# The even mixer's input projection as three products of high and low halves, contraction block outermost

## The chip, the cores and the metric

The kernel runs on one core of a Trainium2 chip. The metric is the device time of one execution in microseconds (us), the median of three runs. Besides these runs there is one profiled execution, from which all rows below come. In the profile PE is the TensorE matmul, PEld its weight load, DVE is VectorE, ACT is ScalarE, POOL is GpSimd and SP is SyncE, which issues most of the transfers.

## The reference

The model has two layers over 384 tokens, 128 context tokens and 256 latent tokens, with 1024 channels. What matters here is the first step of the even layer:

```
h  = x * (1 + scale) + shift              # scale, shift from SiLU(cond) @ ada_w + ada_b
u  = h @ w_in                             # (384 x 1024) @ (1024 x 2048)
ux, ub, uc, up = split(u, 512 columns each)
ya = ub * conv3(uc * ux, conv_w)          # depthwise, width 3
yb = pool_mixer(up, pool_w, pool_scale)   # windowed means minus the token
out = concat(ya, yb) @ w_out
```

After it come a residual with LayerNorm, a dense SwiGLU, the odd layer (latent attention beside a Fourier mixer) and a top-2-of-8 mixture of experts. All inputs are float32.

## The kernel before, in words

Each engine has its own instruction stream, written out by hand, and semaphores tie the streams together. Nothing is planned at run time around the change; the order in each stream is the order of the code.

**Tiles.** `HT` holds the modulated tokens turned, as 8 contraction blocks (`KD` = 8) of 128 channels by 384 tokens. `w_in` comes as four units ("evin", 0 to 3) of 512 columns each, 2 MB a unit, in the order of `EV_ORDER`: first the pooled columns `up`, then `ux`, `ub` and `uc`. The ring `WR` has four slots. Units 0 and 2 lie in slot 3, units 1 and 3 in slot 1. Between them SP loads the 3 MB panels of `ada_w` ("ada", n) and then `w_out` ("evout", 0 and 1). A load into a slot waits until PE has signalled that the slot's last unit is used up (`free`, `release`).

**PE.** `evin(t, ks)` (L2142) multiplies output tile t (128 columns of `w_in` by 384 tokens, one PSUM bank) over the contraction blocks `ks`, in float32. The matmul shows as two records in the trace. The loop from L2167 takes the tiles t = 0 to 15 in turn, all blocks of one tile before the next tile. The first three tiles (`EV_EARLY`) start with blocks 0 to 3, since blocks 4 to 7 of the tokens depend on a later panel: between the first and the second of them stands `ada_turn(2)`. After each unit of four tiles PE does a panel of the modulation (`ada_turn`, L2080, and `ada_mm`, L2106), and after unit 2 also the four matmuls of the pooling mixer (L2190). Then follows `project_out` (L2209).

**ACT.** It modulates the latent tokens in two halves (L1041), then waits for each of the tiles 0 to 11 and copies it out of PSUM (L1048, L1052), then scales the pooled tiles (L1056).

**DVE.** It modulates the context tokens in two halves (L1484), turns the panels into modulation columns (`ada_stage`, L1351 and L1353; `ada_cols`, L1343), multiplies tiles 12 to 15 into the convolution's input (L1503) and does the convolution (L1511 to L1515).

**POOL.** It computes the pooling (L866 to L872) as soon as the tiles 0 to 3 are copied, zeroes rows in memory (L876, L878), stores the first gate (L831) and then loads the LayerNorm gain, bias and the gates (`ln_params(0, 0)`, L841 to L843). It waits for the gate's store alone before these three loads.

**The split products of the feed-forward network.** The SwiGLU that follows already works on halves: ACT casts a weight piece to the rounded type fp32r (the high half, L1065), DVE subtracts it from the float32 piece (the low half, L1538), the same is done with the tokens (L1095, L1554), and `product` (L2240) does three matmuls, high by high, high by low and low by high (L2244 to L2246). Its first two blocks of columns are computed with the contraction block outermost (`first_gate_up`), four PSUM banks in turn.

Of the kernel before, what the change touches and what calls it, by code (L numbers as in the profile page):

```python
# [279 lines left out]
def build(nc, x_prompt, x_sample, cache_ckv, cache_kpe, c, c_ctx, ada_w, ada_b, ln_g, ln_b, ev_w_in, ev_conv_w,  # L280
# [4 lines left out]
    with ctx:  # L285
# [68 lines left out]

        SIL, HF = carve(TOK, TOK)
# [229 lines left out]
        EV_EARLY = 3  # L585
# [36 lines left out]
        def _(sp):  # L622
# [15 lines left out]
            def raw_free(n, more=0):  # L638

                if isinstance(n, int) and n < RING:  # L640
                    return
                sp.wait_ge(lo_done, n - (RING - 1) + more)
# [91 lines left out]
            sp.wait_ge(lo_done, FF_LAST[0] + 1)  # L734
# [88 lines left out]
        def _(pool):  # L823
# [152 lines left out]
        def _(act):  # L976
# [58 lines left out]
            for half in range(2):  # L1035
# [8 lines left out]
            for t in range(12):  # L1044
                act.wait_ge(u_ps, t + 1)
                if t >= 4:
                    dst = (UX, UB)[t // 4 - 1]
                    nc.scalar.copy(dst[:, t % 4, :], PS[:, t % 4, 0:TOK]).then_inc(u_act, 1)  # L1048
                else:
                    act.wait_ge(z_pad, 2)  # L1050
                    for tok, at, n in SEGU:
                        last = nc.scalar.copy(UP[:, t % 4, at:at + n], PS[:, t % 4, tok:tok + n])  # L1052
                    last.then_inc(u_act, 1)
            for g in range(NPOOL):
                act.wait_ge(pm_ps, g + 1)
                nc.scalar.activation(MIX[:, 4 + g, :], PS[:, 4 + g % 2, 0:TOK], ACT.Identity,  # L1056
                                     scale=COLS[:, 12 + g:13 + g]).then_inc(mix_pool, 1)

            def high(piece, used_up):
# [3 lines left out]
                if used_up is not None:  # L1063
                    act.wait_ge(w_used, used_up)
# [255 lines left out]
        def _(dve):  # L1320
# [166 lines left out]

            ada(range(2))
# [45 lines left out]
            def low(piece):  # L1534

                n, at, _ = piece
                dve.wait_ge(hi_done, n + 1)
# [14 lines left out]
            for k in range(KD):  # L1552
                dve.wait_ge(hx_hi, k + 1)
# [500 lines left out]
        def _(pe):  # L2054
# [65 lines left out]
            def release(ins, name):  # L2120


                ins.then_inc(used[ring.units[name][0]], 1)
# [18 lines left out]
            def evin(t, ks):  # L2142

                w = slot(("evin", t // 4))[:, 0:4096].rearrange("p (k n) -> p k n", k=KD)
                for k in ks:
                    last = mm(PS[:, t % 4, 0:TOK], w[:, k, (t % 4) * P:(t % 4 + 1) * P], HT[:, k, :],  # L2146
                              start=(k == 0), stop=(k == KD - 1))
                    if t in (4, 8, 12) and k == 0:
                        release(last, ("ada", 2 + t // 4))
                return last  # L2150
# [7 lines left out]
            pe.wait_ge(ht_a, 1)  # L2158
            pe.wait_ge(ht_d, 1)
            wait_unit(pe, ("evin", 0))  # L2160
            evin(0, range(4))
            ada_turn(2, True)
            for t in range(1, EV_EARLY):
                evin(t, range(4))
            h_ready(0)

            for t in range(16):  # L2167
                if t % 4 == 0 and t:
                    wait_unit(pe, ("evin", t // 4))
                if t >= 4:  # L2170
                    pe.wait_ge(u_act, t - 3)
                evin(t, range(4 if t < EV_EARLY else 0, KD)).then_inc(u_ps, 1)
# [67 lines left out]
            def product(out, left, right, start, stop):  # L2240


                (lh, ll), (rh, rl) = left, right
# [537 lines left out]
```

## Time and profile before

| | us |
|---|---|
| median of three runs | 1333.41 |
| the three runs | 1337.09, 1333.41, 1333.41 |
| profiled execution, its time | 1337.3 |
| profiled execution, its span | 1335.4 |
| PE busy in the span | 1278.3 |
| DVE busy | 715.0 |
| ACT busy | 521.6 |
| POOL busy | 131.2 |

The span is the time from the first to the last instruction. Matmuls are pipelined: the busy time of one lies partly over that of the next, so the pace of a stream is read from the starts of its matmuls and not from their durations. The mean granted TensorE clock is 0.975 of full speed.

### The profile page before, as it was taken

How to read it: one execution, taken by the hardware profiler on the slowest of the kernel's cores; microseconds unless marked ns; L12 is line 12 of the kernel's file. 1: busy time of each engine (PE TensorE's matmuls, PEld its weight loads, DVE VectorE, ACT ScalarE, POOL GpSimd, SP SyncE). 2: the span in 40 equal slices, each digit the busy share in tenths (PEclk: the TensorE clock that was granted, in tenths of full speed). 3: DMA queues.
4: the chain of work that ended last, by engine and by line, in shares of the span. 5: the costliest groups of instructions: out<-in, count | busy, mean ns of one | idle time of the engine just before them, and what ended most of it. 6: DMA issues, size and time to landing. Idle time of an engine off the chain costs nothing.

```text
span 1335.4 us, 17338 instructions
## 1 busy us (share of the span) xinstructions
PE 1278.3 (96%) x6503; PEld 959.3 (72%) x6504; DVE 715.0 (54%) x1026; ACT 521.6 (39%) x632; POOL 131.2 (10%) x119
## 2 busy tenths in 40 slices
PE   4999999999999989999999999999999999999994
PEld 2555449999999964677646886765467878888882
DVE  1101456334234252555335777743256788888888
ACT  0101025233233242234202746533136666777772
POOL 0420003200000033000000010100102021202020
PEclk8999999999999989899998789999999999999997
DMA  9986386424324184720405666859989899999993
GB/s 365 351 340 247 107 319 190 158 95 161 122 94 157 47 320 144 263 78 24 173 0 194 243 228 257 294 193 341 352 317 338 293 338 357 383 366 385 362 358 142
DMA packets 125356, 317.10 MB, mean 237 GB/s; under 512 B 12931, under 2 KB 47078, under 8 KB 124774
## 3 DMA queue, kind: packets, MB, share of 16 engines
q1 hardware_dynamic: 119264, 295.00, 60.7%
q0 software_dynamic: 5744, 21.07, 5.1%
q8 instruction: 43, 0.70, 0.2%
q14 instruction: 27, 0.22, 0.1%
q10 hardware_dynamic: 278, 0.10, 0.0%
HBM read 306.37 MB, written 9.76 MB: 237 GB/s over the span
## 4 chain that ended last, share of the span: by engine, by line
PE 89%; DVE 5%; DMA 3%; issue 1%; SPq 1%; ACT 1%; DVEq 0%; ACTq 0%
PE ps L2546 10%; PE ps L2547 10%; PE ps L2548 10%; PE ps L2244 8%; PE ps L2246 8%; PE ps L2245 8%; PE ps L2209 7%; PE ps L2552 7%; PE ps L2146 6%; PE ps L2336 3%; DMA sb_ring<-in_ev_w_in 2%; PE ps L2106 2%; PE ps L2438 1%; PE ps L2080 1%; DVE sb_expert_lo L1753 1%
## 5 line engine op out<-in xcount | busy, mean ns | idle before, releaser
L1753 DVE TENSOR_TENSOR sb_expert_lo<-sb_expert_raw,sb_expert_hi 128x1792 fp32r<-128x1792 f32 (+1 forms) x210 | 334.1, 1646 | 85.0 <-PE ps L2552 73.7
L1201 ACT CAST sb_expert_hi<-sb_expert_raw 128x1792 fp32r<-128x1792 f32 (+1 forms) x210 | 283.4, 1392 | 117.3 <-PE ps L2548 78.4
L2546 PE MATMUL ps<-sb_expert_hi,sb_expert_x 128*128 128x448 f32 x448 | 166.9, 373 | 4.5 <-DVE sb_expert_lo L1753 2.5
L2547 PE MATMUL ps<-sb_expert_lo,sb_expert_x 128*128 128x448 f32 x448 | 165.3, 369 | 0.0
L2548 PE MATMUL ps<-sb_expert_hi,sb_expert_x 128*128 128x448 f32 x448 | 165.0, 368 | 0.0
L2244 PE MATMUL ps<-sb_split_acts,sb_split_weights 128*128 128x384 f32 x352 | 118.0, 335 | 0.4 <-issue 0.4
L2246 PE MATMUL ps<-sb_split_acts,sb_split_weights 128*128 128x384 f32 x352 | 117.9, 335 | 0.0
L2245 PE MATMUL ps<-sb_split_acts,sb_split_weights 128*128 128x384 f32 x352 | 117.7, 334 | 0.0
L2546 PEld LDWEIGHTS ps<-sb_expert_hi,sb_expert_x 128*128 128x128 f32 x448 | 85.2, 190 | 20.1 <-issue 12.7
L2548 PEld LDWEIGHTS ps<-sb_expert_hi,sb_expert_x 128*128 128x128 f32 x448 | 85.0, 190 | 7.2
L2547 PEld LDWEIGHTS ps<-sb_expert_lo,sb_expert_x 128*128 128x128 f32 x448 | 85.1, 190 | 7.0
L1547 DVE TENSOR_TENSOR sb_scratch<-sb_scratch,ps 128x384 f32<-128x384 f32 x22 | 12.2, 554 | 142.7 <-PE ps L2246 120.4
L1538 DVE TENSOR_TENSOR sb_split_weights<-sb_ring,sb_split_weights 128x1024 fp32r<-128x1024 f32 x66 | 80.7, 1282 | 7.1 <-ACT sb_split_weights L1065 7.1
L2146 PE MATMUL ps<-sb_ht,sb_ring 128*128 128x384 f32 x256 | 83.7, 487 | 0.6 <-DMA sb_ring<-in_ev_w_in 0.6
L2546 PE MATMUL ps<-sb_expert_hi,sb_expert_h 128*128 128x512 f32 x196 | 78.7, 401 | 0.7 <-DVE sb_expert_lo L1753 0.7
L2547 PE MATMUL ps<-sb_expert_lo,sb_expert_h 128*128 128x512 f32 x196 | 77.1, 393 | 0.0
L2548 PE MATMUL ps<-sb_expert_hi,sb_expert_h 128*128 128x512 f32 x196 | 77.1, 393 | 0.0
L2146 PEld LDWEIGHTS ps<-sb_ht,sb_ring 128*128 128x128 f32 x256 | 48.3, 190 | 35.7 <-issue 2.8
L1065 ACT CAST sb_split_weights<-sb_ring 128x1024 fp32r<-128x1024 f32 x66 | 65.1, 1056 | 5.7 <-PE ps L2246 5.7
L2244 PEld LDWEIGHTS ps<-sb_split_acts,sb_split_weights 128*128 128x128 f32 x352 | 66.1, 188 | 1.3 <-issue 0.5
L2245 PEld LDWEIGHTS ps<-sb_split_acts,sb_split_weights 128*128 128x128 f32 x352 | 66.1, 188 | 0.9
L2246 PEld LDWEIGHTS ps<-sb_split_acts,sb_split_weights 128*128 128x128 f32 x352 | 66.1, 188 | 0.0
(339 smaller groups left out, 1835.5 us busy)
## 6 DMA issues: line engine op xcount, KB each, us to landing
sb_expert_raw<-in_moe_w_gate SPq DMA_DIRECT2D x128, 448.0 KB, 5.6
sb_expert_raw<-in_moe_w_up SPq DMA_DIRECT2D x128, 448.0 KB, 7.0
sb_expert_raw<-in_moe_w_down SPq DMA_DIRECT2D x112, 512.0 KB, 7.3
sb_ring<-in_ada_w SPq DMA_DIRECT2D x14, 3072.0 KB, 17.7
sb_ring<-in_ffn_w_gate SPq DMA_DIRECT2D x44, 256.0 KB, 3.8
sb_ring<-in_ffn_w_up SPq DMA_DIRECT2D x44, 256.0 KB, 4.7
sb_ring<-in_ffn_w_down SPq DMA_DIRECT2D x22, 512.0 KB, 6.3
sb_ring<-in_ev_w_in SPq DMA_DIRECT2D x4, 2048.0 KB, 15.4
```

Source lines behind the costliest of these rows:

```text
L1201: nc.scalar.copy(EHI[piece.h][:, 0:w], ERAW[:, r, 0:w]).then_inc(e_hi, 1)
L1538: V.tensor_tensor(WS[:, at, 1, :], RAW[:, at, :], WS[:, at, 0, :].bitcast(F32), ALU.subtract)\
L1753: V.tensor_tensor(ELO[r][:, 0:w], ERAW[:, r, 0:w], EHI[piece.h][:, 0:w].bitcast(F32), ALU.subtract)\
L2146: last = mm(PS[:, t % 4, 0:TOK], w[:, k, (t % 4) * P:(t % 4 + 1) * P], HT[:, k, :], start=(k == 0), stop=(k == KD - 1))
L2209: last = mm(PS[:, 2 * g + h, :], lhs(k)[:, g * P:(g + 1) * P], w[:, k % per, h * 512:(h + 1) * 512], start=(k == 0), stop=(k == n - 1))
L2244: first = mm(out, lh, rh, start=start, stop=False)
L2245: mm(out, lh, rl, start=False, stop=False)
L2246: return first, mm(out, ll, rh, start=False, stop=stop)
L2546: first = mm(out, lh, rh, start=start, stop=False)
L2547: mm(out, lh, rl, start=False, stop=False)
L2548: return first, mm(out, ll, rh, start=False, stop=stop)
L2552: made = [mm(out, left, right, start=start, stop=stop) for out, right in zip(outs, rights)]
```

## The change

The projection of the even mixer is computed with `product` too. ACT casts each of the 8 blocks of tokens to a high half, in the place of the gate rows and the LayerNorm gain (`EVX[0]`), and DVE writes the low half in place over `HT` (`EVX[1]`). Of each weight block (128 by 512) the high half goes to one of four spare places in the unit's own ring slot, and the low half in place over the raw block. The loops of PE are turned: the contraction block is outermost and the four tiles of a unit, in four PSUM banks, innermost. The first pass over blocks 0 to 3 still takes only three tiles, and the fourth follows once the second half of the tokens is ready. ACT may cast block k of 4 to 7 of a unit only once PE has used up block k - 4 (`w_used`). The counters `hi_done`, `lo_done`, `w_used` and `hx_lo`, which the feed-forward network uses, start later by constants. On POOL the loads of `ln_params(0, 0)` wait until all 16 tiles are done.

```diff
+        EVX = tuple(nc.alloc_sbuf_tensor_at(f"sb_input_{part}", [P, KD, TOK], F32R, offset=at)
+                    for part, at in (("hi", gb_at), ("lo", ht_at)))
+        EVW = {at: tuple(nc.alloc_sbuf_tensor_at(f"sb_input_w_{part}{at}", [P, n, 512], F32R, offset=ring_at + 4 * (SLOT * at + col))
+                         for part, n, col in (("hi", 4, 4096), ("lo", KD, 0))) for at in (1, 3)}
+        EV_SPLITS, EV_FREED = 4 * KD, 16
...
@@ ln_params (POOL)
+                else:
+                    pool.wait_ge(u_ps, 16)
...
@@ ACT
+            def input_high(half):
+                act.wait_ge(ht_a, half + 1)
+                act.wait_ge(ht_d, half + 1)
+                for k in range(4 * half, 4 * half + 4):
+                    nc.scalar.copy(EVX[0][:, k, :], HT[:, k, :]).then_inc(hx_hi, 1)
+            def input_w_high(u, ks):
+                for k in ks:
+                    if k == 0:
+                        wait_unit(act, ("evin", u))
+                    if k >= 4:
+                        act.wait_ge(w_used, 4 * u + k - 3)
+                    hi, _, raw = input_w(u, k)
+                    nc.scalar.copy(hi, raw).then_inc(hi_done, 1)
...
+            modulate_sample(0)
+            input_high(0)
+            input_w_high(0, range(4))
+            modulate_sample(1)
+            input_high(1)
+            input_w_high(0, range(4, KD))
+            for u in range(1, 4):
+                input_w_high(u, range(4))
+                input_out(u - 1)
+                if u == 3:
...
+                input_w_high(u, range(4, KD))
...
@@ DVE
+            def input_w_low(u, ks):
+                for k in ks:
+                    dve.wait_ge(hi_done, KD * u + k + 1)
+                    hi, lo, raw = input_w(u, k)
+                    V.tensor_tensor(lo, raw, hi.bitcast(F32), ALU.subtract).then_inc(lo_done, 1)
             ada(range(2))
             modulate_prompt(0)
-            ada(range(2, 3))
+            input_low(0)
+            ada_stage(2)
+            input_w_low(0, range(2))
+            ada_cols(2)
+            input_w_low(0, range(2, 3))
             modulate_prompt(1)
+            input_w_low(0, range(3, 4))
+            input_low(1)
+            input_w_low(0, range(4, KD))
+            input_w_low(1, range(4))
             ada_stage(3)
+            input_w_low(1, range(4, KD))
             ada_cols(3)
+            input_w_low(2, range(4))
             ada_stage(4)
+            input_w_low(2, range(4, KD))
             ada_gate(0, 5)
             ada_cols(4)
+            input_w_low(3, range(4))
             ada_stage(5)
+            input_w_low(3, range(4, KD))
...
@@ PE
-            def evin(t, ks):
-                w = slot(("evin", t // 4))[:, 0:4096].rearrange("p (k n) -> p k n", k=KD)
-                for k in ks:
-                    last = mm(PS[:, t % 4, 0:TOK], w[:, k, (t % 4) * P:(t % 4 + 1) * P], HT[:, k, :],
-                              start=(k == 0), stop=(k == KD - 1))
+            def evin(u, k, tiles=range(4)):
+                pe.wait_ge(lo_done, KD * u + k + 1)
+                if u == 0:
+                    pe.wait_ge(hx_lo, k + 1)
+                hi, lo, _ = input_w(u, k)
+                for t in tiles:
+                    if u and k == 0:
+                        pe.wait_ge(u_act, 4 * u + t - 3)
+                    cols = slice(t * P, (t + 1) * P)
+                    first, last = product(PS[:, t, 0:TOK], (hi[:, cols], lo[:, cols]), (EVX[0][:, k, :], EVX[1][:, k, :]),
+                                          k == 0, k == KD - 1)
...
+                    if k == KD - 1:
+                        last.then_inc(u_ps, 1)
+                if k < 4 and t == 3:
+                    last.then_inc(w_used, 1)
             ada_mm(2)
-            evin(0, range(4))
+            evin(0, 0, range(3))
             ada_turn(2, True)
-            for t in range(1, EV_EARLY):
-                evin(t, range(4))
+            for k in range(1, 4):
+                evin(0, k, range(3))
             h_ready(0)
-            for t in range(16):
...
+            for k in range(4):
+                evin(0, k, (3,))
+            for t in range(3, 16, 4):
+                for k in range(4 if t == 3 else 0, KD):
+                    evin(t // 4, k)
```

## Rows read from the trace of the kernel before

**Rows 1.** The page, busy time of the engines: us, share of the span, instructions.

```profile
PE 1278.3 (96%) x6503; PEld 959.3 (72%) x6504; DVE 715.0 (54%) x1026; ACT 521.6 (39%) x632; POOL 131.2 (10%) x119
```

**Rows 2.** Chain of waits up to 240 us: start, duration, what held the chain.

```profile
12.93 26.58 DMA sb_ring<-in_ev_w_in
39.65 2.82 PE ps L2146 x8
...
61.86 2.72 PE ps L2106 x32
64.58 20.84 PE ps L2146 x64
...
117.51 20.65 PE ps L2146 x64
138.19 0.63 DVE sb_scratch L1503 x2
...
147.44 13.93 PE ps L2209 x32
```

**Rows 3.** Stretches of the four units, L2146 alone: stretch, busy by engine, PEclk, DMA.

```profile
39.65:61.86 22.21, 21.12 (x64) 11.97 (x64) 1.00 1.01 375
sum 84.54, PE 83.43 PEld 47.79; mean PE 20.86 PEld 11.95
```

**Rows 4.** PE in order of time in the feed-forward network: start, duration, matmul.

```profile
215.06 0.33 PE L2244 MATMUL ps<-sb_split_acts,sb_split_weights 128*128 128x384 f32 x1
...
220.26 0.39 PE L2244 MATMUL ps<-sb_split_weights,sb_split_hidden 128*128 128x512 f32 x1
```

**Rows 5.** Groups by line and shape, weight loads, 203 to 260 us.

```profile
L2245 PEld LDWEIGHTS ps<-sb_split_acts,sb_split_weights 128*128 128x128 f32 x80 | 15.0, 188 | 0.1
```

**Rows 6.** Four stretches, PE alone: stretch, busy, PEclk (granted clock), DMA share, GB/s.

```profile
203.50:210.00 6.50, 6.46 (x37) 1.00 0.69 196
485.00:492.00 7.00, 5.14 (x24) 0.55 1.03 362
...
200.00:204.00 4.00, 2.40 (x23) 1.00 0.65 191
```

**Rows 7.** One line each, ACT and DVE: duration ns min/median/max, first and last start.

```profile
L1065 ACT CAST sb_split_weights<-sb_ring x26: 1037/1049/1159, 202.1 to 299.5; 128x1024 fp32r<-128x1024 f32 x26
L1095 ACT CAST sb_split_acts<-sb_ht x8: 615/622/628, 201.3 to 207.0; 128x384 fp32r<-128x384 f32 x8
L1538 DVE TENSOR_TENSOR sb_split_weights<-sb_ring,sb_split_weights x24: 1215/1219/3416, 203.3 to 298.9; 128x1024 fp32r<-128x1024 f32 x24
L1554 DVE TENSOR_TENSOR sb_split_acts<-sb_ht,sb_split_acts x8: 550/552/559, 201.9 to 209.1; 128x384 fp32r<-128x384 f32 x8
```

**Rows 8.** DVE in order of time, 39 to 45 us.

```profile
43.73 0.17 DVE L1343 TENSOR_TENSOR sb_mod_cols<-ps,sb_mod_bias 128x12 f32<-128x12 f32 x1 [4.07 <-PE ps L2080]
43.94 1.37 DVE L1484 TENSOR_SCALAR sb_ht<-ps,sb_mod_cols 128x128 f32<-128x128 f32 x4
```

**Rows 9.** POOL in order of time: first and last pooling step, an LN load.

```profile
52.30 0.87 POOL L866 TENSOR_TENSOR sb_scratch<-sb_scratch 128x415 f32<-128x415 f32 x1 [15.19 <-ACT sb_scratch L1052]
...
70.73 1.26 POOL L872 TENSOR_TENSOR sb_scratch<-sb_scratch 128x128 f32<-128x128 f32 x2
...
114.28 0.53 POOL L843 DMA_DIRECT2D sb_gate_rows<-gate_rows  x1
```

**Rows 10.** Transfers by issue: KB each, us to landing (the last LN load).

```profile
sb_gate_rows<-gate_rows POOLq DMA_DIRECT2D x1, 1024.0 KB, 14.3
```

**Rows 11.** The issue of unit 1 at 33.5 us: issue, and its time to landing.

```profile
L630 SPq DMA_DIRECT2D sb_ring<-in_ev_w_in x1: 2601/2601/2601, 33.5 to 33.5; - x1
DMA to landing us min/median/max: 22.6/22.6/22.6
```

**Rows 12.** DVE, L1538 while POOL works, 222 to 230 us: duration ns min/median/max.

```profile
L1538 DVE TENSOR_TENSOR sb_split_weights<-sb_ring,sb_split_weights x2: 3187/3302/3416, 222.7 to 225.8; 128x1024 fp32r<-128x1024 f32 x2
```

**Rows 13.** The issue of evout 1 at 140 us: issue, and its time to landing.

```profile
L630 SPq DMA_DIRECT2D sb_ring<-in_ev_w_out x1: 368/368/368, 140.2 to 140.2; - x1
DMA to landing us min/median/max: 7.8/7.8/7.8
```

More of the change, by code:

```diff
@@ L1033, in squares, with modulate_sample @@
                     .then_inc(sd_ready, 1)
-            for half in range(2):
+            def modulate_sample(half):
                 act.wait_ge(xt_t, 2 * NG)
@@ L1043, in _ @@
                 last.then_inc(ht_a, 1)
[L1044 to L1053, printed above, removed]
@@ new lines, in input_w_high, with input_out @@
+            def input_w_high(u, ks):
[6 more added lines that the diff above has]
+                    nc.scalar.copy(hi, raw).then_inc(hi_done, 1)
+            def input_out(u):
+                for t in range(4 * u, 4 * u + 4):
+                    act.wait_ge(u_ps, t + 1)
+                    if u:
+                        dst = (UX, UB)[u - 1]
+                        nc.scalar.copy(dst[:, t % 4, :], PS[:, t % 4, 0:TOK]).then_inc(u_act, 1)
+                    else:
+                        act.wait_ge(z_pad, 2)
+                        for tok, at, n in SEGU:
+                            last = nc.scalar.copy(UP[:, t % 4, at:at + n], PS[:, t % 4, tok:tok + n])
+                        last.then_inc(u_act, 1)
@@ new lines, in _ @@
+            modulate_sample(0)
[8 more added lines that the diff above has]
+                if u == 3:
+                    for g in range(NPOOL):
+                        act.wait_ge(pm_ps, g + 1)
+                        nc.scalar.activation(MIX[:, 4 + g, :], PS[:, 4 + g % 2, 0:TOK], ACT.Identity,
+                                             scale=COLS[:, 12 + g:13 + g]).then_inc(mix_pool, 1)
+                input_w_high(u, range(4, KD))
@@ L2141, in _, with product @@
             pe.wait_ge(sc_ready, 1)
-            def evin(t, ks):
-                w = slot(("evin", t // 4))[:, 0:4096].rearrange("p (k n) -> p k n", k=KD)
-                for k in ks:
-                    last = mm(PS[:, t % 4, 0:TOK], w[:, k, (t % 4) * P:(t % 4 + 1) * P], HT[:, k, :],
-                              start=(k == 0), stop=(k == KD - 1))
-                    if t in (4, 8, 12) and k == 0:
-                        release(last, ("ada", 2 + t // 4))
-                return last
+            def product(out, left, right, start, stop):
+                (lh, ll), (rh, rl) = left, right
+                first = mm(out, lh, rh, start=start, stop=False)
+                mm(out, lh, rl, start=False, stop=False)
+                return first, mm(out, ll, rh, start=False, stop=stop)
+            def evin(u, k, tiles=range(4)):
[9 more added lines that the diff above has]
+                                          k == 0, k == KD - 1)
+                    if u and (t, k) == (0, 0):
+                        release(first, ("ada", 2 + u))
+                    if k == KD - 1:
+                        last.then_inc(u_ps, 1)
+                if k < 4 and t == 3:
+                    last.then_inc(w_used, 1)
             ada_mm(0)
@@ L2237, in _ @@
             h_ready(1)
-            def product(out, left, right, start, stop):
-                (lh, ll), (rh, rl) = left, right
-                first = mm(out, lh, rh, start=start, stop=False)
-                mm(out, lh, rl, start=False, stop=False)
-                return first, mm(out, ll, rh, start=False, stop=stop)
             def halves(buf, *at):
```

42 lines of the change are left out of this document (19 added, 23 removed).

## Prediction

> **What bounds the kernel now.** I read the busy times first: PE is at work in 96% of the span, DVE in 54%, ACT in 39%, POOL in 10% [rows 1]. So only what shortens PE's own stream, or a wait of PE, moves the time. Next the chain of waits up to 240 us: from 39.65 us, when the first unit of `w_in` has landed, to 138.16 us it is PE alone, four units of projection (the last takes 20.65 us) with panels between (2.72 us for 32 records of `ada_mm`) [rows 2]. Then comes a short stretch on DVE, which prepares the convolution, and PE goes on with `project_out` at 147.44 us. Third the stretches of the four units: their matmuls keep PE busy for 83.43 us, at full granted clock in the one shown [rows 3]. That is the term the change works on. There are 16 tiles x 8 blocks = 128 float32 matmuls in it, so one costs 83.43 / 128 = 0.652 us.
>
> **What three products cost.** The same shape (128x128 weights, 384 columns, fp32r) runs in the feed-forward network. From the matmul that starts at 215.06 us to the one at 220.26 us there are 30 of them, ten products of three [rows 4]: 5.20 / 30 = 0.173 us a matmul, 0.520 us a product. The printed 0.33 us is the latency of one, of which half lies under its neighbour; three times that would be 1.0 us and would forecast a loss, and it is not the pace. 128 products take 66.6 us. PE saves 83.4 - 66.6 = 16.9 us.
>
> The bounds of this term: if the weight load sets the pace, at 188 ns a load [rows 5], the 384 matmuls take 72.2 us and the saving is 11.2. Those loads too start every 0.173 us in the feed-forward stream, or the pace of rows 4 could not hold, so I take 0.173.
>
> The new loop goes through four PSUM banks in each block. The stretch 203.5 to 210 us has that very order (`first_gate_up`), and its granted clock is 1.00, the 2.4 GHz level [rows 6]. The Trainium skill speaks against the order: its page "TensorE: Matmul & The Clock Gate", section "A second HAM failure mode: psum-queue depth-cycling", says that going through banks in each iteration can leave small idle times that make the clock swing between its levels. By the row the products cost 66.6 us; by the rule a part of them would run at half clock (a rival below). By the rule, this trace doesn't agree: the row shows no swing.
>
> **The splits.** There are 32 casts and 32 subtractions of 128x512, and 8 of each of 128x384. Casts take 0.622 us at 384 and 1.049 at 1024 columns, subtractions 0.552 and 1.219 [rows 7]; in between, 0.71 and 0.69 us for 512. ACT gets some 28 us of work and DVE some 26 us, over the 84 us of the stretch, in which DVE and ACT are mostly idle. PE takes 4 x 0.520 = 2.08 us for a block, each splitter 0.7, so in the steady state the halves are ready early: block k + 4 may be cast when block k is used up, which leaves it 3 x 2.08 = 6.2 us for 0.33 + 0.71 + 0.69 = 1.7 us of work. They cost nothing there. If that cover were gone, each of the 16 blocks with k of 4 to 7 would put up to 1.7 us on PE.
>
> *At the start* nothing covers them. The unit lands at 39.6 us; PE now waits for the first cast and subtraction, 0.71 + 0.69 = 1.4 us. Nearest rows from both sides: 1.17 (two ops of 384 columns) and 2.27 (two of 1024) [rows 7]. I take 1.4. The tokens' halves 0 to 3 are done before the weights land.
>
> *The rest of unit 0.* PE: block 0 on three tiles to 42.6, `ada_turn(2)` to 43.8, blocks 1 to 3 on three tiles by 48.5. DVE's `ada_cols(2)` was at 43.73 and comes near there again, then one subtraction, then the context half, 1.37 us [rows 8], then block 3's subtraction, ready at some 46.9; PE wants it at 46.9. The fourth tile's blocks 0 to 3 run 48.5 to 50.6, and block 4's cast waits for the first of them: 48.5 + 0.52 + 0.33 + 0.71 + 0.69 = 50.75. I put 0.25 us on this unit; the bounds are 0 and 1.0 (one split more in front). It then ends at 59.1 instead of 61.8.
>
> *Unit ends.* All four tiles now finish within the last 2.1 us of a unit, and the next unit's first block wants the banks copied out. ACT's copies are below 0.622 us each [rows 7], four are below 2.5 us, the first starts 1.2 us before the end, and PE has 2.72 us of `ada_mm` at least between units [rows 2]. Nothing is added while ACT is not held up. But ACT now stands at unit u + 1's first cast ahead of the copies of unit u. Unit 1 landed at 33.5 + 22.6 = 56.1 us [rows 11], four casts end by 59, and the first copy is due at 57.9: late by 1.1, inside the panel. Units 2 and 3 have 10 us more slack, since their issue moves forward with PE.
>
> *DVE's order.* `ada_cols(3)` and `ada_cols(4)`, which wait for PE's panels, now have the next unit's first subtractions queued behind them. `ada_cols(3)` comes 2.72 us before unit 2 starts, enough for three of 0.69 us. Cost 0. What waits behind the new waits for `hi_done` is `ada_stage`, used only after the next unit.
>
> *POOL beside DVE.* The pooling lay at 52.3 to 72.0 us [rows 9]; with all four tiles copied only after unit 0 it starts some 6 us later and runs beside unit 1's subtractions. While POOL worked, L1538 took 3.19 to 3.42 us instead of 1.22 [rows 7, 12]. A subtraction of 512 would then take up to 1.7 to 2 us. DVE does one per 2.08 us of PE there, with four blocks of lead: cost 0. The Trainium skill, "GPSIMD Engine Reference", section "Key points", says that GpSimd shares its SBUF interfaces with VectorE and contends with instructions that have two SBUF inputs, as these subtractions have. Its rule and the row agree on the stretching; it weighs in a rival below.
>
> *After unit 3.* The four products into the convolution's input (0.63 us a tile [rows 2]) were spread over the unit; now they come at its end, 0.52 us apart. The last ends about 1.1 us after PE instead of 0.65. I put 0.45 us, with bounds 0 and 1.9 (three of them wholly late).
>
> *POOL's new wait.* The LayerNorm loads move behind unit 3's end, the last from 114.3 to some 124 us. The last took 14.3 us and landed at 128.6 [rows 9, 10]; now at 138. What reads it is the residual after the first third of `project_out`, which ends at 147.44 + 13.93 = 161.4 before, 146.6 then. 8 us remain. What queues behind it is only the second gate's store. These loads now run beside evout 1, issued 2 us after unit 3 and landed 7.8 us later [rows 13]: 125.1 + 7.8 = 132.9 alone. With all 14.3 us in front of it, 139.4; its rows are wanted halfway through the first 13.93 us of `project_out`, at 139.6. Cost 0, bound 2.
>
> **Sum.** -16.9 + 1.4 + 0.25 + 0.45 = -14.8 us. After 138 us every wait, load and store is timed from PE's progress, so the gain goes through. The profiled execution took 1337.3 us (span 1335.4), which gives 1322.5. It stands 3.9 above the median of the runs; that is the highest of the three too, 1337.09. From the median, 1333.4 - 14.8 = 1318.6.
>
> **Rivals.**
> *One clock dip at the start.* PE's pause before unit 0 grows by 1.4 us. The stretch 485 to 492 us, in which PE was busy for 5.14 of 7 us, ran at a granted clock of 0.55 [rows 6]: 7 x 0.45 = 3.2 us lost, 1321.8. Against it stands 200 to 204 us, busy for 2.40 of 4 us and at 1.00.
> *The weight load sets the pace:* 5.6 us more, 1324.2.
> *Late halves.* ACT and DVE are in-order queues; with the spare high places freed by PE, the cast after that and the subtraction last (stretched beside POOL), PE could end in step with them on the 16 late blocks. At 0.7 us a block 11.2 us are lost, 1329.8, no change. At the full 1.73 it is 27.7, which gives +12.9 and 1346.3: slower. It decides from 14.8 / 16 = 0.93 us a block. For it speaks only the row of 3.4 us; against it the lead of 6.2 us, and that POOL's work ends in unit 2.
> *The clock swings* between 1.2 and 2.4 GHz through the products: at half the time slow, 33 us more, 1352. This is what the row 203.5 to 210 speaks against. By the rule of the Trainium skill's page "TensorE: Matmul & The Clock Gate" cited above, this is the outcome.
>
> **How the numbers follow.** Forecast 0.76, dip 0.09, weight load 0.03, late halves shallow 0.03 (still faster) and 0.04 (no change), in step 0.03, swinging clock 0.02. A measurement can tell 0.3%, 4 us, from no change. Faster: 0.76 + 0.09 + 0.03 + 0.03 = 0.91; same 0.04; slower 0.05. The range: the low end is the whole 16.9 us and 2 us of luck with clock dips elsewhere, 1314.5; the high end takes in the dip and the weight-load pace with 1 us, 1325.5.
>
> **What would show it.** Starts of L2245 0.173 us apart in the units; each of units 1 to 3 lasting 16.6 us; PE's pause before unit 0 longer by 1.4 us; the first `ada_mm` after unit 0 at 59 and unit 3's end at 123 us; no wait of PE for the halves longer than 0.3 us; granted clock 1.00. It would be wrong if idle time before PE's products sums to more than 3 us, if the pace is 0.19, or if a later stage (evout 1, the gate rows) begins to wait.

## The result, and the profile after

| | before | after |
|---|---|---|
| median, six runs each, us | 1335.25 | 1326.41 |
| lowest and highest, us | 1331.6, 1339.34 | 1324.09, 1328.77 |
| profiled execution: time, span, mean clock | 1337.3, 1335.4, 0.975 | 1324.09, 1322.3, 0.971 |
| project_out starts in the profile, us | 147.4 | 134.4 |

The ratio of the runs is 0.9928, with a 95% interval of 0.9906 to 0.9951: 8.8 us faster, where 14.8 were forecast. 1326.4 lies just above the range, which ended at 1325.5. With all the runs of this study the changed kernel has a median of 1326.9 (18 runs) and the kernel before one of 1337.4 (125 runs, 1330.2 to 1341.9), so the gain is 10.5 us. The 1333.4 from which the forecast started was the median of three favourable runs; 4.0 us of the miss in absolute time come from there, and 4.3 from the gain.

The chain of waits of the changed kernel up to 135 us (start, duration, what held the chain) answers to [rows 2].

```profile
38.32 0.52 ACT sb_input_hi L1066
38.86 1.28 DVE sb_input_lo L1540 x3
40.27 0.55 DVE sb_input_lo L1540
40.83 0.47 DVE sb_mod_stage L1399
41.29 0.47 DVE sb_mod_stage L1401
41.76 0.61 DVE sb_input_w_lo L1547
42.41 0.45 PE ps L2219
...
60.86 2.72 PE ps L2180 x32
...
123.87 2.01 DVE sb_scratch L1577 x7
...
134.49 13.93 PE ps L2294 x32
```

Ahead of unit 0 the chain isn't the landing any more. It goes through the token halves, then the two panel copies, then the first low half of the weights, all on DVE and one behind the other. The first product starts at 42.41 us, 2.76 us after the 39.65 of the kernel before.

The units themselves, PE alone (stretch, busy, PEclk, DMA share, GB/s), answer to [rows 3].

```profile
42.41:60.79 18.38, 18.38 (x109) 1.00 1.04 385
63.50:80.27 16.77, 16.77 (x100) 1.00 0.81 310
84.31:101.07 16.76, 16.76 (x101) 1.00 1.03 388
108.08:125.02 16.94, 16.94 (x99) 1.00 0.62 246
```

Units 1 to 3 take 16.8 to 16.9 us instead of 20.7 to 20.8. Unit 0 holds a part of a panel besides its products (18.4 us, 22.2 before). The pace is the forecast one, as the starts of PE in order of time show (start, duration, matmul):

```profile
50.14 0.33 PE L2219 MATMUL ps<-sb_input_hi,sb_input_w_hi 128*128 128x384 f32 x1
50.31 0.33 PE L2220 MATMUL ps<-sb_input_lo,sb_input_w_hi 128*128 128x384 f32 x1
50.48 0.33 PE L2221 MATMUL ps<-sb_input_hi,sb_input_w_lo 128*128 128x384 f32 x1
50.66 0.33 PE L2219 MATMUL ps<-sb_input_hi,sb_input_w_hi 128*128 128x384 f32 x1
```

0.52 us for a product, 0.173 us a matmul. The groups by line and shape from 38 to 140 us (busy, mean ns, idle before) show the splits and the only idle time of PE before a product:

```profile
L2219 PE MATMUL ps<-sb_input_hi,sb_input_w_hi 128*128 128x384 f32 x128 | 43.6, 341 | 1.3 <-DVE sb_input_w_lo L1547 1.3
...
L1547 DVE TENSOR_TENSOR sb_input_w_lo<-sb_ring,sb_input_w_hi 128x512 fp32r<-128x512 f32 x32 | 21.8, 714 | 24.9 <-ACT sb_input_w_hi L1076 24.9
L1076 ACT CAST sb_input_w_hi<-sb_ring 128x512 fp32r<-128x512 f32 x32 | 18.3, 619 | 32.3 <-PE ps L2221 26.2 <-DMA sb_ring<-in_ev_w_in 6.1
```

In this profile the start of project_out has moved by 12.95 us and the span by 13.1. So the single pair of profiles shows 13 of the forecast 14.8 us, and the medians 10.5. The pair flatters the change: the changed kernel's profiled execution, 1324.1, is the fastest of its first six, and that of the kernel before, 1337.3, is a usual one. The granted clock differs too: the changed kernel's 18 runs have a mean clock of 0.970, and those of the kernel before (119 whose clock is on record) 0.973.

### The profile page after: what moved, and what is told of

Read it like the earlier page. It is cut to its first block, busy times and chain, and to the rows that moved or that the text cites. A ratio compares the mean times of both kernels' runs of the same rounds, so it can differ in the third digit from the quotient of the medians.

```text
span 1322.3 us, 17688 instructions
## 1 busy us (share of the span) xinstructions
PE 1265.0 (96%) x6631; PEld 979.9 (74%) x6632; DVE 739.4 (56%) x1066; ACT 543.4 (41%) x672; POOL 132.6 (10%) x119
## 4 chain that ended last, share of the span: by engine, by line
PE 89%; DVE 5%; DMA 3%; issue 1%; ACT 1%; SPq 0%; DVEq 0%; ACTq 0%
PE ps L2623 10%; PE ps L2219 10%; PE ps L2624 10%; PE ps L2625 10%; PE ps L2221 10%; PE ps L2220 10%; PE ps L2294 7%; PE ps L2629 7%; PE ps L2413 3%; PE ps L2180 2%; PE ps L2154 2%; DMA sb_ring<-in_ada_w 1%; PE ps L2515 1%; DVE sb_expert_lo L1827 1%; PE ps L2511 1%
## 5 line engine op out<-in xcount | busy, mean ns | idle before, releaser
L2221 PEld LDWEIGHTS ps<-sb_split_acts,sb_split_weights 128*128 128x128 f32 x352 | 66.6, 189 | 0.0
L928 POOL TENSOR_TENSOR sb_scratch<-sb_constants 1x1 f32<-1x1 f32 x19 | 18.1, 953 | 466.3 <-DVE sb_static_rows L1850 297.7
```

Of the source, the lines that this page charges most:

```text
L2221: return first, mm(out, ll, rh, start=False, stop=stop)
```

## The experiments

"Tail" is the time from project_out's first matmul to the end of the span. "Half clock" is the time in the tail at the 1.2 GHz level, summed from the trace's record of the granted clock. Both are of the profiled execution. The median is of all runs of that kernel, and so is the last column: the half-clock time in the whole span, worked out for each run from its span and mean clock, 2 x (1 - clock) x span, and averaged. "Runs beside it" are those of the kernel before that were made together with a version and to which its ratio refers; their medians lie between 1336.9 and 1338.4 us.

| kernel (labels) | median (runs) | unit 0 starts | panel after unit 0 | project_out | tail | half clock | half clock, whole span, all runs |
|---|---|---|---|---|---|---|---|
| before | 1337.4 (125) | 39.65 | 61.79 | 147.37 | 1188.1 | 57.8 | 71.3 |
| before again (e2) | | 40.93 | 63.11 | 148.69 | 1189.4 | 65.4 | |
| before, third (e15) | | 39.76 | 61.98 | 147.56 | 1190.6 | 66.0 | |
| before, fourth (e16) | | 41.25 | 63.42 | 149.00 | 1189.4 | 65.1 | |
| after | 1326.9 (18) | 42.41 | 60.79 | 134.42 | 1187.8 | 59.6 | 79.6 |
| after again (e1) | | 40.95 | 62.49 | 136.13 | 1189.8 | 65.3 | |
| after, third (e11) | | 42.51 | 60.91 | 134.55 | 1189.4 | 61.3 | |
| order only (e3) | 1336.9 (12) | 41.32 | 63.49 | 149.07 | 1189.6 | 65.4 | 71.4 |
| pause only (e10) | 1335.5 (12) | 42.59 | 64.74 | 150.32 | 1183.8 | 47.4 | 63.6 |
| before + filler (e6) | 1333.6 (12) | 39.02 | 61.17 | 146.75 | 1184.8 | 52.8 | 57.1 |
| after + filler (e5) | 1321.8 (6) | 40.28 | 60.21 | 133.85 | 1185.6 | 53.5 | 65.1 |
| after, DVE order (e8) | 1323.2 (12) | 41.64 | 60.04 | 133.68 | 1188.2 | 62.2 | 71.8 |
| the same again (e12) | | 41.61 | 60.01 | 133.66 | 1186.0 | 56.1 | |
| block 0 float32 (e4) | 1319.4 (10) | 39.02 | 57.88 | 131.52 | 1184.0 | 49.9 | 65.1 |
| the same again (e7) | | 41.37 | 60.23 | 133.86 | 1184.1 | 47.9 | |
| block 0 float32 + filler (e9) | 1321.3 (6) | 38.98 | 57.81 | 131.45 | 1181.9 | 45.8 | 63.8 |
| after + 1.3 us of work (e13) | 1326.0 (6) | 41.17 | 59.58 | 134.61 | 1183.7 | 46.6 | 71.5 |
| after + 2.6 us of work (e14) | 1325.2 (6) | 40.88 | 62.47 | 138.79 | 1181.4 | 42.4 | 69.7 |
| block 0 float32 + 1.3 us (e17) | 1323.9 (6) | 39.32 | 58.18 | 133.22 | 1188.9 | 61.3 | 74.5 |

The tail goes with its half-clock time. A straight line through the 19 profiles is 1166.2 + 0.36 x half clock, and no profile lies more than 1.0 us off it. The seven profiles of the kernel before and its versions and the twelve of the changed kernel and its versions lie on the same line (mean distance 0.0 for both). So no later stage got slower for good with the change: at the same half-clock time the tail is as long as before.

**e1 and e11, the changed kernel again.** No edit.

> The changed kernel once more, for a second profile and more times. The first profiles differ by 13.1 us in span, the medians by 8.8. Theory C (clock): the work of PE is shortened by 13 us, and 3 to 5 us of it are given back in single executions by stretches at half clock (mean granted clock 0.969 to 0.971 in the changed kernel's runs, 0.975 in the profile of the kernel before). Then PE reaches project_out at 134.5 +- 1 us again, the times lie at 1324 to 1329, and a longer run has a lower mean clock: about 1.3 us for each 0.001. Rival N (noise of few runs): the gain of the medians moves to 12 or 13 us with more runs. Rival O (another stage got slower for good): the second profile shows a stage outside the projection that is longer by several us at full clock.

> The changed kernel a third time, for a third profile. Theory: either PE starts unit 0 late (42.4 us, panels at half clock, order on DVE) or in time (41 us) and runs its first blocks at half clock; both ways the panel after unit 0 starts at 60.8 to 62.5 us where my sum had 59.1, and project_out at 134.4 to 136.2. Median 1327 +- 1. If the start is not the cause, this profile shows a panel at 59.1 +- 0.5 us and still a time of 1325 or more.

e1: median 1327.6, ratio 0.9925 (0.9909 to 0.9941). e11: 1326.3, ratio 0.9926 (0.9904 to 0.9948). The first result was no accident, the noise rival falls. What I had not expected is what e1 shows at the start. PE alone, two stretches (stretch, busy, PEclk, DMA share, GB/s), first in e1:

```profile
24.00:41.00 17.00, 13.52 (x89) 0.70 1.04 392
41.00:49.00 8.00, 8.00 (x32) 0.57 1.02 374
```

and in the first profile of the changed kernel:

```profile
24.00:41.00 17.00, 15.80 (x88) 0.51 1.04 392
41.00:49.00 8.00, 6.66 (x46) 1.00 1.03 376
```

There are two ways to lose. Either the panels before unit 0 run at half clock, the tokens are modulated later, and PE starts at 42.4 us. Or PE starts at 40.95, 1.4 us after the landing as in my sum, and its first blocks run mostly at half clock: the clock is 0.57 from 41 to 49 us, ahead of which PE had paused for 1.95 us. The panel after unit 0 starts at 60.8, 60.9 and 62.5 us where the sum had 59.1. e13 and e14 have the same start, and their profiles add to this: e14 repeats e1 (pause of 1.95 us, clock 0.57, panel at 62.5), while e13 loses in neither way. There PE paused longest, 3.65 us, and the clock stayed up in unit 0, as this stretch of PE alone shows:

```profile
41.00:49.00 8.00, 7.83 (x49) 1.00 1.03 376
```

Its unit 0 starts at 41.17 and its panel at 59.6, nearly as forecast. So the length of the pause doesn't say whether the clock falls after it; what does is open.

**e2, e15, e16, the kernel before again.** No edit.

> The kernel before once more, for a second profile. Theory C: the places and number of half-clock stretches differ from the first profile (31 to 39 us, 486, 544, 725, 752, 776, 1315, 1325 us), the span by up to 4 us, all of it inside such stretches; project_out starts at 147.4 +- 1. Rival N: the span comes out near 1333 to 1336 and the clock does not explain the differences. The ratio of its times to the kernel before is 1.000 +- 0.002.

> The kernel before a third time, for a third profile: where its project_out starts (147.4 and 148.7 so far) and how long its tail is (1188.1 and 1189.4). If the tail of the kernel before is the same as the changed kernel's on the average, project_out must start at 146.5 or so for the medians to differ by 10.5 only; by theory T its mean tail is 2 to 3 us shorter, so here 1184 to 1187 with less than 57 us of half-clock time.

> The kernel before a fourth time, same question and same numbers.

Its four profiles have project_out at 147.4 to 149.0, 148.2 on the average; the changed kernel's three have 134.4 to 136.1, 135.0. So 13.1 us are gained there. The two tails of 1190.6 and 1189.4 miss what I had expected of e15 and e16. But the three profiled executions of e2, e15 and e16 lie at the slow end of their own runs (1340 us against a median of 1337.4), so they say little about the usual tail. From the medians, less the 1.8 us that an execution's time lies above its span, the usual tail is 1337.4 - 1.8 - 148.2 = 1187.4 us before and 1326.9 - 1.8 - 135.0 = 1190.1 after. That is worked out, not seen.

**e3, the order of the loops alone**, in float32.

```diff
-            for t in range(16):
-                if t % 4 == 0 and t:
+            for k in range(4):
+                evin(0, k, (3,))
+            for t in range(3, 16, 4):
+                if t > 3:
                     wait_unit(pe, ("evin", t // 4))
...
-                evin(t, range(4 if t < EV_EARLY else 0, KD)).then_inc(u_ps, 1)
+                for k in range(4 if t == 3 else 0, KD):
+                    evin(t // 4, k)
```

> One part of the change alone: the loops of the projection are turned (contraction block outermost, four banks), with float32 matmuls on the unsplit tokens and weights, no splits and no later LayerNorm loads. If the order by itself costs something (rival: bank switching, tiles that finish together), units 0 to 3 take longer than 20.9 us each and the kernel is slower than before by 1 us or more. By my sum the order costs only the convolution's input at the end: +0.2 to +0.5 us, units at 20.9 us, time within 1 us of the kernel before.

Median 1336.9, ratio 0.9993 (0.9977 to 1.0009). PE alone in units 1 to 3:

```profile
66.21:86.95 20.74, 20.74 (x68) 1.00 0.83 320
91.00:111.74 20.74, 20.74 (x68) 1.00 0.65 247
119.05:139.69 20.64, 20.64 (x66) 1.00 0.75 299
```

As expected: going through four banks costs nothing and the clock stays at 1.00. The Trainium skill, "TensorE: Matmul & The Clock Gate", section "A second HAM failure mode: psum-queue depth-cycling", describes a bfloat16 kernel whose clock swings when it goes through the banks in each iteration. This case's traces don't show that, neither in float32 (1.00 here) nor in the products (1.00 in the four units above).

**e5 and e6, a filler in PE's idle time** ahead of the second panel, in the changed kernel and in the one before.

```diff
             x_turned(0)
+            for _ in range(7):
+                mm(PS[:, 6, 0:384], ident, X[:, 0, 0:384], start=True, stop=True)
             ada_mm(1, None, 0)
```

> The changed kernel with seven more float32 matmuls (128x128 by 128x384, some 0.65 us each, into a PSUM range that the next panel overwrites) in PE's idle time between the turned tokens and the landing of the second panel (19.5 to 24.4 us). Theory C (clock): the half-clock stretches between 24 and 41 us, and the one at 42 to 49 us that one profile of the changed kernel shows, come from this idle time and from the pause before unit 0. With the filler the clock stays at 1.00 up to about 39 us, the panels before unit 0 end at 38 us, PE starts the first product 1.0 to 2.0 us earlier than in the changed kernel's profiles (40.95 and 42.41 us), project_out starts at 132.5 to 134, and the median falls by 1.5 to 3 us. Rival (the landing of unit 0 and the order on DVE alone hold the start): project_out starts at 134.4 or later and the median moves by less than 1 us.

> The same filler in the kernel before. There PE waits for the landing of unit 0 at 39.6 us whatever its clock was, unless it is late (40.93 us in one profile). Theory C: the first matmul of unit 0 starts at 39.6 us, project_out at 147.4 us; the median falls by 0 to 1.3 us, less than in the changed kernel, since the float32 matmuls hang on the landing alone. Rival (the clock lottery is the same for both kernels and has nothing to do with the start): both kernels move by the same amount.

e5: 1321.8, ratio 0.9899 (0.9875 to 0.9922). e6: 1333.6, ratio 0.9981 (0.9964 to 0.9998). In e5, PE alone:

```profile
24.00:33.00 9.00, 5.99 (x57) 1.00 1.03 398
33.00:41.00 8.00, 5.20 (x35) 0.76 1.04 384
41.00:49.00 8.00, 8.00 (x44) 0.82 1.03 376
```

The filler holds the clock at 1.00 to 33 us, and later it still falls twice. The three profiles with the filler (e5, e6, e9) have 3.4 to 6.8 us at half clock ahead of unit 0, the sixteen without it 10.2 to 20.5. The start gets better by 1.2 to 1.4 us in both kernels, against the averages of their profiles. But the medians fall by 5.1 and 3.8 us, more than the start explains. In the kernel before I had expected at most 1.3; against the runs beside it the fall is 2.5 us, and its interval, 0.3 to 4.8, does not exclude that. The rest is in the tails, 1185.6 and 1184.8.

**e8 and e12, another order on DVE before unit 0.**

```diff
-            input_low(0)
-            ada_stage(2)
-            input_w_low(0, range(2))
+            input_low(range(1))
+            input_w_low(0, range(1))
+            ada_stage(2)
+            input_low(range(1, 4))
+            input_w_low(0, range(1, 2))
```

> The changed kernel with another order on DVE before unit 0: low half of token block 0, low half of weight block 0, then the panel copies (ada_stage of panel 2), then the low halves of token blocks 1 to 3. Theory S (the order on DVE holds the start): PE's first product starts at 41.0 us at either clock level, up to 1.4 us earlier than in the profile with 42.4; project_out starts 0.5 to 1.4 us earlier and the median is 0.5 to 1.5 us lower than the changed kernel's 1327.3. Rival: PE reaches unit 0 only at 41.0 us when its clock is halved, so the order on DVE gives at most 0.3 us, and the wait moves behind block 0, to the panel copies.

> The other order on DVE once more: its six times spread from 1316 to 1327 us. Theory S: the median stays 2 to 5 us under the changed kernel's, PE starts unit 0 within 0.3 us of the end of its panel or 1.4 us behind the landing, whichever is later. Rival: the first median of 1323.2 was luck, and it is back at 1326 or more.

1323.2, ratio 0.9895 (0.9865 to 0.9925), and 1322.9, ratio 0.9899 (0.9876 to 0.9923). DVE in order of time in e8:

```profile
39.13 0.56 DVE L1540 TENSOR_TENSOR sb_input_lo<-sb_ht,sb_input_hi 128x384 fp32r<-128x384 f32 x1 [1.20 <-ACT sb_input_hi L1066]
40.89 0.69 DVE L1547 TENSOR_TENSOR sb_input_w_lo<-sb_ring,sb_input_w_hi 128x512 fp32r<-128x512 f32 x1 [1.20 <-ACT sb_input_w_hi L1076]
41.50 0.55 DVE L1399 COPY sb_mod_stage<-ps 128x384 f32<-128x384 f32 x1
41.97 0.55 DVE L1401 COPY sb_mod_stage<-ps 128x384 f32<-128x384 f32 x1
```

The first low half of the weights comes 0.9 us earlier than the 41.8 of the changed kernel, the panel copies go under the products, and PE starts at 41.6. The panel after unit 0 starts at 60.0 instead of 60.8. So the order on DVE did hold the start. It gives 3.7 us in the median, 0.8 us of it ahead of project_out (133.7 against 134.5 at the same early clock).

**e4, e7 and e9, block 0 of unit 0 in float32**, with and without the filler.

```diff
+                if (u, k) == (0, 0):
+                    for t in tiles:
+                        last = mm(PS[:, t, 0:TOK], input_w(0, 0)[2][:, t * P:(t + 1) * P], HT[:, 0, :], start=True, stop=False)
+                    if t == 3:
+                        last.then_inc(w_used, 1)
+                    return
...
             input_w_low(0, range(4, KD))
+            dve.wait_ge(w_used, 1)
+            input_low(range(1))
```

> The changed kernel with block 0 of unit 0 multiplied in float32 from the unsplit tokens and weights, so that PE needs no halves to start; the token block is split after that for units 1 to 3. Theory S (start): in the changed kernel PE started its first product at 42.4 us, 2.8 us after the landing, held by the chain of token halves, panel copies and first weight halves on DVE. Then PE starts at 39.6 to 41.1 us here, pays 4 x 0.13 us more for the block, and project_out starts 1 to 2 us earlier than in the changed kernel, the time is 1 to 2 us lower. Rival: the start is not what is missing, later waits in unit 0 (the tokens' second half, block 4) take the time back, and project_out starts within 0.4 us of the changed kernel's 134.5.

> The kernel with block 0 of unit 0 in float32 once more, since its four times lay 8 us below the changed kernel where its start explains 3 to 4.5 us (project_out at 131.5 instead of 134.4 and 136.1). Theory C: the other 4 to 5 us were shorter half-clock stretches (mean clock 0.976 instead of 0.9695), which depend on the pauses of PE before unit 0 for 1 or 2 us and on luck for the rest, so the median rises to 1320 to 1323. Rival: the float32 start changes the later stretches for good, and the median stays at 1319 +- 1 with a clock of 0.976.

> Both remedies at once: block 0 of unit 0 in float32, and the seven filler matmuls at 19.5 us. Theory C: the clock is mostly at 1.00 before unit 0 and PE starts at the landing, 39.0 to 39.6 us, in each execution, so project_out starts at 131.5 +- 0.5 and the median is 0 to 2.5 us under the 1319.7 of float32 block 0 alone. Rival (each remedy repairs the same loss, the rest is luck of the clock): 1319.7 +- 1.

1319.0 and 1319.7, ratios 0.9872 (0.9851 to 0.9894) and 0.9877 (0.9851 to 0.9903), all ten runs 1319.4: the fastest version here, 18.0 us under the kernel before. PE no longer waits for a half before unit 0: it starts at the landing (e4, 39.0) or when its own panel ends (e7, 41.4). The start of project_out is 131.5 or 133.9, by the clock before 41 us. Again the median gains more (7.5 us on the changed kernel) than the start (0.6 to 4.6), and the tails are short, 1184. e9, with both remedies, has the shortest span of all in its profile (1313.3) and yet no better median, 1321.3 (1315.2 to 1324.8), ratio 0.9895 (0.9873 to 0.9917).

**e10, the pause alone.** The kernel before, with a copy and a subtraction between the landing and PE's first matmul; their results are not used.

```diff
+                if half == 0:
+                    wait_unit(act, ("evin", 0))
+                    nc.scalar.copy(SCR[:, 0:512], slot(("evin", 0))[:, 0:512]).then_inc(pause_a, 1)
...
+            dve.wait_ge(pause_a, 1)
+            V.tensor_tensor(SCR[:, 512:1024], slot(("evin", 0))[:, 0:512], SCR[:, 0:512], ALU.subtract).then_inc(pause_d, 1)
...
+            pe.wait_ge(pause_d, 1)
```

> The kernel before with the start's pause alone: after the landing of unit 0 ACT copies its first block and DVE subtracts it, both into scratch that nothing reads, and PE waits for the subtraction before its first float32 matmul. Nothing is computed from them. By my sum the pause costs its own 1.4 us: project_out at 148.8 to 149, time +1.4 us. Theory C (a longer pause before unit 0 brings half-clock time after it, as in the second profile of the changed kernel): project_out at 149 to 151, the median 2 to 5 us above the kernel before, the mean clock lower by 0.001 to 0.003. Rival (pause hidden since PE's panel ends at 41 us in most executions): +0 to +0.7 us.

Median 1335.5, ratio 0.9995 (0.9982 to 1.0008), that is -2.4 to +1.1 us against the runs beside it. This contradicts my sum (+1.4) and theory C (+2 to +5). The time would allow the rival's +0 to +0.7, but its reason, a hidden pause, is not what the profile shows: PE starts unit 0 at 42.59 us and project_out at 150.3, 2.1 us behind the average of the kernel before and the latest of all. The tail is 1183.8 us, 4 to 7 us shorter than in the kernel before. It isn't this one execution alone: over the twelve runs the half-clock time is 63.6 us on the average, against 70.0 in the runs beside them. With this the theory "lost at the start" falls as a full account: what happens ahead of project_out is not what arrives at the end.

**e13, e14 and e17, known work ahead of project_out.** Two or four matmuls whose results are not used.

```diff
                     ada_mm(7, None, 6)
+                    pe.wait_ge(mix_pool, 4)
+                    for _ in range(2):
+                        mm(PS[:, 5, 0:384], ident, X[:, 0, 0:384], start=True, stop=True)
```

> The changed kernel with two more float32 matmuls (128 by 384, 0.65 us each, results unused) right ahead of project_out. In 14 profiles so far the time from the start of project_out to the end lies between 1181.9 and 1189.8 us and goes with the half-clock time in it (45.8 to 65.4 us); the changed kernel's three are all long (1187.8 to 1189.8). Theory T (the tail is set by where PE's later pauses fall on the clock's own steps, and a small shift of PE's schedule moves it): 1.3 us of added work does not show as +1.3 us; half-clock time in the tail changes by 5 us or more and the median moves to anywhere between -2.5 and +2.5. Rival (each us ahead of project_out is a us at the end, and the missing 2 to 3 us have another cause): +1.3 +- 0.4 us, half-clock time in the tail stays at 60 to 65 us.

> The same with four such matmuls, 2.6 us. Rival: +2.6 +- 0.4 us, 1329.4. Theory T: not proportional to the work added, a median of 1325 to 1328 and a tail that is shorter by 1 us or more than the changed kernel's 1189.

> The kernel with block 0 in float32, and two more float32 matmuls (1.3 us, results unused) right ahead of project_out. In the changed kernel, whose tail was long, 1.3 us of added work cost nothing (median 1326.0 against 1326.9). Here the tail is short already (1184.0 and 1184.1 us in two profiles). Theory T: a shift can only make it as long or longer, so the median rises by 1.3 us or more, to 1321 to 1325. Rival (the short tail comes with the float32 start itself, whatever follows): 1319.7 + 1.3 = 1321.0 +- 0.7, tail 1185.3 with the added work in front of it, that is 1184 after it.

Added to the changed kernel, 1.3 us of work gives 1326.0 (ratio 0.9911, 0.9888 to 0.9934) and 2.6 us gives 1325.2 (0.9911, 0.9884 to 0.9939): 0.9 and 1.7 us less than without. Added to the kernel with block 0 in float32, the same 1.3 us gives 1323.9 (0.9907, 0.9885 to 0.993): 4.5 us more. Each median is of six runs that spread over 5 to 8 us, so the two small gains are not certain. That the work isn't simply paid for is safer: 1326.9 + 1.3 and 1326.9 + 2.6 lie above the highest of the six runs of e13 and of e14, and 1319.4 + 1.3 lies below the lowest of e17.

Where it happens: PE alone in three stretches of the tail. The profiled execution of e13 (1320.2) was the fastest of its six, so it shows what a fast execution looks like and not the version's usual one; those of e7 (1319.9) and e17 (1324.0) lie at their medians. In the changed kernel

```profile
470.00:485.00 15.00, 11.68 (x84) 0.77 1.03 373
530.00:545.00 15.00, 13.93 (x63) 0.77 0.85 317
710.00:750.00 40.00, 37.76 (x206) 0.70 0.71 273
```

in e13

```profile
470.00:485.00 15.00, 11.67 (x99) 0.89 1.02 359
530.00:545.00 15.00, 13.20 (x74) 0.89 0.82 309
710.00:750.00 40.00, 37.50 (x226) 0.83 0.82 317
```

in e7

```profile
470.00:485.00 15.00, 11.68 (x80) 0.89 1.04 379
530.00:545.00 15.00, 14.24 (x75) 0.89 0.96 362
710.00:750.00 40.00, 37.75 (x212) 0.79 0.81 311
```

and in e17:

```profile
470.00:485.00 15.00, 12.37 (x76) 0.77 1.04 379
530.00:545.00 15.00, 15.00 (x73) 0.77 0.95 365
710.00:750.00 40.00, 37.76 (x198) 0.70 0.72 275
```

The instructions of the tail are the same. The clock falls at the same places: at the end of the feed-forward network, where PE has waited 2.6 us for DVE, in the odd layer, and ahead of the experts. The last, the longest (20.5 us in the changed kernel), follows no pause of PE. It begins at 713.1 us, within the router's small matmuls, while PE is busy in all of the time (changed kernel; PE in order of time, then two stretches of PE alone):

```profile
710.57 8.12 PE L2557 MATMUL ps<-sb_router,sb_ht 128*128 128x8 f32 x48
708.00:713.00 5.00, 5.00 (x54) 1.00 1.01 357
717.00:725.00 8.00, 8.00 (x39) 0.50 1.03 409
```

In each place the clock stays down for different times. A clock of 0.70 over 40 us is 40 x 2 x 0.30 = 24 us at half clock, 0.83 is 13.6. The table's extremes are 42.4 us at half clock with a tail of 1181.4, and 66.0 with 1190.6: 0.39 us for each, near the 0.36 of the line through all.

## Why the prediction was wrong

**Right: the pace.** 0.173 us a matmul, no limit from the weight loads, no swing in the four-bank order (e3), no wait for halves in units 1 to 3. Of the saving of 16.65 us (16.9 less the 0.25 of unit 0) 15.7 are there, from the 84.54 us of [rows 3] to the 68.85 of the four stretches: units 1 to 3 take 0.1 to 0.3 us more than 32 products at 0.520. The splits were costed at 0.71 and 0.69 us and measured 0.62 and 0.68, the subtraction up to 1.05 beside POOL, as in this line of DVE in order of time:

```profile
66.56 1.00 DVE L1547 TENSOR_TENSOR sb_input_w_lo<-sb_ring,sb_input_w_hi 128x512 fp32r<-128x512 f32 x1 [2.37 <-ACT sb_input_w_hi L1076]
```

**Right: POOL's later loads.** They were issued from 125.5 us, and evout 1, issued at 127.2, took 13.0 us instead of the 7.8 of [rows 13]: it landed at 140.2. By my sum it was wanted at 139.6, so it would have been late by 0.6 us; since project_out began at 134.4 and not at 132.6, its 17th matmul, the first to use these rows, came at 141.4, and PE didn't wait. In e4, where project_out began at 131.5, it landed at 137.6 and was wanted at 138.5. From the end of unit 3 to project_out it is 9.4 us, 9.3 before; the 0.45 us for the convolution's input was at most 0.2.

**Wrong: "The tokens' halves 0 to 3 are done before the weights land", and with it the 1.4 us of the start and the 0.25 us of unit 0.** I counted the cast and the subtraction of the first weight block and left out what stands in front of them in DVE's queue: the token halves until 40.8, then the panel copies until 41.8. When the panels run at half clock the chain ends at 42.4, 2.76 us after the start in the kernel before, where the sum had 1.4. When they don't, the clock can fall after the pause (e1 and e14, not e13), the rival to which I gave 0.09. The panel after unit 0 came 1.7, 1.8 and 3.4 us later than the 59.1 of my sum. Against the average of the four profiles before (62.6) unit 0 brought 1.2 us, not 2.7. e4, e7, e8 and e12 show the term by removing it: with the panels at half clock, as in the profile with 134.4, project_out starts at 133.9 (e7) and 133.7 (e8, e12).

**Wrong: "After 138 us every wait, load and store is timed from PE's progress, so the gain goes through."** The loads are, the clock isn't. 13.1 us are gained at project_out (averages of three and four profiles) and 10.5 at the end. e10, e13, e14 and e17 show that a shift of 1.3 to 3 us ahead of project_out changes the half-clock time (last column of the table), and the end moves by anything from -2 to +4.5 us. The changed kernel's missing 2.6 us are of this kind, as far as the numbers go: over all its runs it is at half clock for 79.6 us, the kernel before for 71.3. Of this the profiles have 17.1 and, on the average of four, 14.5 us ahead of project_out, which leaves 62.5 and 56.8 us behind it. By the line through the 19 profiles that is 2.1 us of tail. This is an estimate from means, not a pair of profiles, since three of the four of the kernel before were of its slower executions. What decides, in a given schedule, how long the clock stays down stays open.

**The base.** The forecast time was built on a median of three runs, 4 us below that of 125. I took the profiled execution, at 1337.3, for a slow one; it was the usual one.

**A slip in a rival.** The 33 us of the swinging clock hold if half of the products run at half clock. At half the time, as I wrote, it is 66.6 / 0.75 = 88.8 us, 22 more. The rival did not come true, so nothing hangs on it.

## What to carry to other kernels

When a step puts a preparation in front of the first matmul, count the queue in front of that preparation on its engine, not its own duration; here a first block in float32 from the unsplit data, during which the halves of the next blocks are made, removed the wait and made the fastest version, 1319.4 us. Compare the starts of matmuls and not their durations to price a product of halves: 0.520 us for three against 0.652 for one in float32. And where the clock falls in several later places, a change of 1 to 3 us early on can't be read off the total: take several profiles, compare the start of a later stage, compare the mean clock of all runs, and add a known amount of work to see whether it arrives.

## What the runs showed of the hardware

The half-clock time behind project_out varied from 42.4 to 66.0 us over 19 profiles of nearly the same instructions, and the tail with it from 1181.4 to 1190.6 us. Known work of 1.3 us ahead of it changed the median by -0.9 us in one kernel and by +4.5 in another. The longest half-clock stretch of the changed kernel (20.5 us, from 713.1) began while PE was busy without a pause, and in e13 a pause of 3.65 us before unit 0 was followed by none to 49 us, where in e1 and e14 one of 1.95 us was. Seven matmuls in an idle time of 5 us at 19.5 us held the clock at 1.00 to 33 us; without them it was 0.51 and 0.70 from 24 to 41 us in two profiles of the changed kernel. And 17.1 us at half clock ahead of unit 0 instead of 10.2 cost the kernel before only 1.3 to 1.6 us (unit 0 at 40.9 or 41.3 instead of 39.7), since PE was waiting for the landing anyway.
